# Keys of the cross attention by products with the weights stationary, and a second input scaled on GpSimd before its transposes

## The reference, cut to what matters

```python
h = rmsnorm(x, norm_xattn_g[i])
m = rmsnorm(mem.astype(dt), norm_mem_g[i])
q = (h @ xattn_wq[i].astype(dt)).reshape(bsz, seq, XATTN_HEADS, XATTN_HEAD_DIM)
k = (m @ xattn_wk[i].astype(dt)).reshape(bsz, -1, XATTN_HEADS, XATTN_HEAD_DIM)
v = (m @ xattn_wv[i].astype(dt)).reshape(bsz, -1, XATTN_HEADS, XATTN_HEAD_DIM)
s = jnp.einsum('bshd,bmhd->bhsm', q, k).astype(f32) * (XATTN_HEAD_DIM ** -0.5)
p = jax.nn.softmax(s, axis=-1).astype(dt)
o = jnp.einsum('bhsm,bmhd->bshd', p, v).reshape(bsz, seq, D_MODEL)
```

## Time and profile before

| what | value |
|---|---|
| median of the runs | 1251.29 us |
| profiled execution, its own time | 1251.01 us |
| span of the profiled execution | 1249.8 us |
| TensorE busy | 1240.9 us, 99% of the span |
| VectorE busy | 814.7 us |
| ScalarE busy | 691.5 us |
| GpSimd busy | 140.7 us |
| granted TensorE clock, mean | 0.999 of full speed |

### The profile page before, as it was taken

The page is one execution under the profiler, slowest core; times in us unless marked ns, Lnnn a source line. Parts: engine busy times, 40 slices in busy tenths (PEclk is TensorE's granted clock), DMA queues, the critical chain, the costliest instruction groups (busy, mean ns, idle before and its releaser), DMA issues.

```text
span 1249.8 us, 17456 instructions
## 1 busy us (share of the span) xinstructions
PE 1240.9 (99%) x7066; PEld 1032.7 (83%) x7066; DVE 814.7 (65%) x1114; ACT 691.5 (55%) x1046; POOL 140.7 (11%) x119
## 2 busy tenths in 40 slices
PE   9999999999999999999999999999999999999997
PEld 7888888888888888888888887888888888888886
DVE  5657755566788556655567878746875765755654
ACT  6665644443778645444447765556855364655543
POOL 1130000000231200000000332000320000211112
PEclk9999999999999999999999999999999999999999
DMA  8755466865454657655545534333456543565652
GB/s 299 230 155 185 149 222 202 267 187 163 151 164 160 215 156 250 195 178 180 177 153 186 184 120 150 122 104 101 136 197 240 170 151 126 168 218 174 205 171 85
DMA packets 127697, 220.18 MB, mean 176 GB/s; under 512 B 8336, under 2 KB 71184, under 8 KB 127616
## 3 DMA queue, kind: packets, MB, share of 16 engines
q1 hardware_dynamic: 123360, 205.95, 51.1%
q0 software_dynamic: 2672, 10.20, 2.4%
q10 hardware_dynamic: 1584, 2.92, 0.6%
HBM read 215.88 MB, written 3.15 MB: 175 GB/s over the span
## 4 chain that ended last, share of the span: by engine, by line
PE 96%; issue 1%; DMA 1%; ACT 1%; DVE 0%; POOL 0%; ACTq 0%; SPq 0%; POOLq 0%
PE ps L403 25%; PE ps L405 25%; PE ps L404 25%; PE ps L503 5%; PE ps L507 2%; PE ps L823 1%; PE ps L420 1%; PE ps L680 1%; PE ps L811 1%; PE ps L1076 1%; PE ps L1061 1%; PE ps L782 0%; DMA ar<-in_mem 0%; PE ps L610 0%; DMA raw<-in_w_gate_up 0%
## 5 line engine op out<-in xcount | busy, mean ns | idle before, releaser
L1618 DVE TENSOR_TENSOR spl<-raw,spl 128x1024 fp32r<-128x1024 f32 x387 | 476.7, 1256 | 100.4 <-ACT spl L1109 99.0
L1109 ACT CAST spl<-raw 128x1024 fp32r<-128x1024 f32 x387 | 400.1, 1050 | 177.4 <-PE ps L405 88.3
L403 PE MATMUL ps<-spl,xs 128*128 128x512 f32 x928 | 371.5, 400 | 0.0
L405 PE MATMUL ps<-spl,xs 128*128 128x512 f32 x928 | 362.4, 391 | 0.0
L404 PE MATMUL ps<-spl,xs 128*128 128x512 f32 x928 | 361.8, 390 | 0.0
L405 PEld LDWEIGHTS ps<-spl,xs 128*128 128x128 f32 x928 | 174.3, 188 | 37.1
L403 PEld LDWEIGHTS ps<-spl,xs 128*128 128x128 f32 x928 | 174.5, 188 | 35.6 <-issue 1.5
L404 PEld LDWEIGHTS ps<-spl,xs 128*128 128x128 f32 x928 | 174.7, 188 | 34.1 <-issue 0.5
L403 PE MATMUL ps<-spl,ys 128*128 128x512 f32 x496 | 198.5, 400 | 0.1
L405 PE MATMUL ps<-spl,ys 128*128 128x512 f32 x496 | 193.7, 391 | 0.0
L404 PE MATMUL ps<-spl,ys 128*128 128x512 f32 x496 | 193.4, 390 | 0.0
(11 more groups left out here) (329 smaller groups left out, 1152.2 us busy)
## 6 DMA issues: line engine op xcount, KB each, us to landing
raw<-in_w_in SPq DMA_DIRECT2D x112, 512.0 KB, 3.9
raw<-in_w_gate_up SPq DMA_DIRECT2D x176, 256.0 KB, 4.0
raw<-in_mlp_w SPq DMA_DIRECT2D x64, 512.0 KB, 4.4
raw<-in_w_down SPq DMA_DIRECT2D x44, 512.0 KB, 4.4
raw<-in_w_out SPq DMA_DIRECT2D x24, 512.0 KB, 4.2
raw<-in_xattn_wk SPq DMA_DIRECT2D x8, 512.0 KB, 3.9
raw<-in_xattn_wv SPq DMA_DIRECT2D x8, 512.0 KB, 4.4
raw<-in_w_branch_gdn SPq DMA_DIRECT2D x8, 512.0 KB, 3.3
```

The lines of the kernel that those rows point to most:

```text
L403: self.do.matmul(bank, xh, hi, start=start, stop=False)
L405: m = self.do.matmul(bank, xl, hi, start=False, stop=stop)
L1109: self.do.copy(self.k.spl[:, u % NH, 0, :], self.k.raw[:, u % NR, :]).then_inc(*self.up("hi", (u,)))
L1618: self.do.tensor_tensor(lo, self.k.raw[:, u % NR, :], hi.bitcast(F32), ALU.subtract).then_inc(*self.up("lo", (u,)))
```

## The change

Keys: `kept()` no longer makes the two key blocks with tokens on partitions. A new `keys(i)` makes each from four `cols_joined` units (of 512 x 256 instead of 256 x 512 weights), and after every second one `key_sums` copies one half of PSUM on ScalarE and adds the other on VectorE. So what is stored and loaded back already has features on partitions, `kept_turn` with its 16 transposes is gone, and the scores wait for the load. The stores of the two key blocks come one step later.

Second input: joined products have the rows of `mem2` on the free axis, where a factor for each row can't be applied while PSUM is emptied. So `mem2` itself is scaled: at step 2 ScalarE takes the squares, VectorE adds the epsilon and GpSimd takes the power and multiplies the 128 x 1024 tile, for each of the two row tiles. The transposes at steps 6 and 7 wait for that. The squares at step 8 are gone, and the values are copied instead of scaled when PSUM is emptied.

```diff
     def xa_scores(self, p, t):
-        self.wait_ge(*self.at("am", "xt", "k", p, 1))
+        self.wait_ge(*self.at(f"ld_kv{p}", 0))
...
     def keep(self, i):
-        self.wait_ge(*self.at("ev", f"x{i}", 1))
+        if i < 2:
+            self.wait_ge(*self.at("dm", f"xk{i}", 1, 1))
+        else:
+            self.wait_ge(*self.at("ev", f"x{i}", 1))
...
+    def mem2_scale(self, t):            # ScalarE
+        self.wait_ge(*self.at("ld_mem2", 0))
+        self.fresh("sqm")
+        if t:
+            self.wait_ge(*self.at("sq", "mem2", 0))
+        self.do.activation(self.s("sqm"), self.s(f"mem2{'ab'[t]}"), ACT.Square,
+                           accum_out=self.small(f"ss_mem2{t}", 1)).then_inc(*self.up("sq", ("mem2", t)))
+
+    def key_sums(self, i, p):           # ScalarE
+        for f in range(2):
+            self.wait_ge(*self.at("mm", f"xk{i}", p, f))
+            self.fresh(f"x{i}")
+            self.do.copy(self.s(f"x{i}")[:, (2 * p + f) * T:(2 * p + f + 1) * T],
+                         self.ps((f"xk{i}", p), f)[:, T:2 * T]).then_inc(*self.up("am", ("xkc", i, p, f)))
...
+    def mem2_scale(self, t):            # VectorE
+        self.factor("mem2", t)
+
+    def key_sums(self, i, p):           # VectorE
+        for f in range(2):
+            c = self.s(f"x{i}")[:, (2 * p + f) * T:(2 * p + f + 1) * T]
+            self.wait_ge(*self.at("am", "xkc", i, p, f))
+            self.do.tensor_tensor(c, self.ps((f"xk{i}", p), f)[:, 0:T], c, ALU.add).then_inc(*self.up("dm", (f"xk{i}", p, f)))
...
+    def mem2_scale(self, t):            # GpSimd
+        v = self.s(f"mem2{'ab'[t]}")
+        self.factor("mem2", t)
+        self.wait_ge(*self.at("rs", "mem2", t))
+        self.do.tensor_tensor(v, v, self.small(f"r_mem2{t}", 1).to_broadcast([P, D]), ALU.mult).then_inc(*self.up("pm", ("mem2", t)))
...
     def second():
+        E.take("sqm")
+        for t in range(2):
+            E.mem2_scale(t)
+        E.give("sqm", ("sq", "mem2", 1))
+        yield
         for p in range(4):
-            E.turn_in("mem2", lambda E, t, p: (E.s(f"mem2{'ab'[t]}"), ("ld_mem2", 0)), p)
+            E.turn_in("mem2", lambda E, t, p: (E.s(f"mem2{'ab'[t]}"), ("pm", "mem2", t)), p)
             if p % 2:
                 yield
         for t in range(2):
-            E.squares_in("mem2", lambda E, t, p: (E.s(f"mem2{'ab'[t]}"), ("ld_mem2", 0)), t, f"mem2{'ab'[t]}")
-            E.give(f"mem2{'ab'[t]}", ("sq", "mem2", t))
-        yield
+            E.give(f"mem2{'ab'[t]}", ("tp", "in", "mem2", 3))
+
+    def keys(i):
+        for p in range(2):
+            for k in range(2):
+                E.cols_joined((f"xk{i}", p), at_half(W["xattn_wk"], 512 * i + 256 * p), k, "ys", tiles("mem2"))
+                if k:
+                    if not p:
+                        E.take(f"x{i}")
+                    E.key_sums(i, p)
+                E.ahead()
+                if i and (p, k) == (0, 0):
+                    keep(0)
+                yield
...
-         (second(), (6, 7, 8)), (ma, (15, 16, 17, 19, 22, 22, 25, 27, 29)), (norm, (29, 30, 31, 32)),
+         (second(), (2, 6, 7)), (ma, (15, 16, 17, 19, 22, 22, 25, 27, 29)), (norm, (29, 30, 31, 32)),
...
-        for i, n in enumerate(("xk0", "xk1", "xv0", "xv1")):
+        for i, n in enumerate(("xkT0", "xkT1", "xv0", "xv1")):
...
-    def kept_turn():
-        E.take("xkT0", "xkT1")
-        for i in range(2):
-            E.xa_turn("k", i, f"xk{i}", (f"ld_kv{i}", 0))
-            E.give(f"xk{i}", ("mx", "xt", "k", i, 1))
-            yield
...
-    plan(opening(E, "m1", W["w_branch_gla"], "xs", turned("yb")), (kept_turn(), (3, 4)))
+    plan(opening(E, "m1", W["w_branch_gla"], "xs", turned("yb")))
```

More of the change, by code:

```diff
@@ L1166, in evac @@
             self.fresh(blk)
-            self.wait_ge(*self.at("rs", n, t))
-            self.do.mul(self.s2(blk)[:, t, :], self.ps(blk, t),
-                        self.small(f"r_{n}{t}", 1)).then_inc(*self.up("ev", (blk, t)))
+            if n == "mem2":
+                a = self.do.copy(self.s2(blk)[:, t, :], self.ps(blk, t))
+            else:
+                self.wait_ge(*self.at("rs", n, t))
+                a = self.do.mul(self.s2(blk)[:, t, :], self.ps(blk, t), self.small(f"r_{n}{t}", 1))
+            a.then_inc(*self.up("ev", (blk, t)))
+    def mem2_scale(self, t):
[11 more added lines that the diff above has]
+                         self.ps((f"xk{i}", p), f)[:, T:2 * T]).then_inc(*self.up("am", ("xkc", i, p, f)))
     def squares(self, tag, v, n, ready, name):
@@ L2352 @@
 ahead turn turn_in squares_in norm_prep norm_scale rows_half acc_done evac gated gate_evac relu squares sums power factors merge let_merged
-up_sum up_relu warm load_first first_half load_ident load_rows load_tables load_second load_con load_gain load_slot load_kept load_narrow load_gate half weights keep
+up_sum up_relu mem2_scale key_sums warm load_first first_half load_ident load_rows load_tables load_second load_con load_gain load_slot load_kept load_narrow load_gate half weights keep
 mem_keys mem_keys_turn ma_norm ma_turn ma_scores softmax ma_sums eight ma_eight ma_out out_norm
@@ L2973, in second, with keep @@
         for t in range(2):
-            E.squares_in("mem2", lambda E, t, p: (E.s(f"mem2{'ab'[t]}"), ("ld_mem2", 0)), t, f"mem2{'ab'[t]}")
-            E.give(f"mem2{'ab'[t]}", ("sq", "mem2", t))
-        yield
+            E.give(f"mem2{'ab'[t]}", ("tp", "in", "mem2", 3))
[11 more added lines that the diff above has]
+                yield
+    def keep(i):
+        E.keep(i)
+        E.give(f"x{i}", (f"ld_st{i}", 0))
     def kept():
-        for i in range(4):
-            w = W["xattn_wv" if i > 1 else "xattn_wk"]
-            for k, _ in enumerate(block(E, f"x{i}", w, 512 * (i % 2), "ys", "mem2")):
+        for i in range(2):
+            yield from keys(i)
+        for i in range(2, 4):
+            for k, _ in enumerate(block(E, f"x{i}", W["xattn_wv"], 512 * (i % 2), "ys", "mem2")):
                 if k == 3:
-                    E.keep(i)
-                    E.give(f"x{i}", (f"ld_st{i}", 0))
+                    keep(i)
+                elif i == 2 and not k:
+                    keep(1)
                 yield
```

## The result

The changed kernel takes 1257.1 us (median of 6 runs, 1255.89 to 1258.21) against 1251.49 us for the kernel before (6 runs, 1250.8 to 1252.2): the ratio is 1.0043, with an interval of 1.0032 to 1.0055. It is slower by 0.4%, 5.6 us, where the forecast had 3.7 us. The profiled execution took 1257.37 us, with a span of 1256.1 us against 1249.8.

What follows compares the result with a forecast made beforehand. The prediction took TensorE's stream, busy 1240.9 of 1249.8 us, as the bound. Its terms, -1.74 + 0.3 + 4.0 + 1.1 = +3.7 us, gave 1255.0 us; own range 1253.3 to 1257, 8 in 10 1249.8 to 1258.3.

Steps and rivals of the forecast that it cites:

- The stream of TensorE: TensorE's own work: 16 transposes removed, -1.74 us, and 8 joined key units, +0.3 us; net -1.4 us.
- The scaling ahead of the transposes: Scaling `mem2` at step 2 delays GpSimd's and VectorE's work, so TensorE stalls 4.0 us, bounds 1.7 and 6.8.
- The prediction's own sign: Test on the changed kernel: no TensorE wait for GpSimd at step 6 (2 to 3 us expected) means the forecast is wrong.
- The splits are made four steps ahead, so that by itself costs nothing: VectorE's split of step 3 runs 2.9 us later, no sooner than 334.4, at no cost by itself.
- What TensorE meets at steps 6, 7 and 10: TensorE waits 2.5 us at `mem2`'s transposes; its shift is 3.4 us after group 0 and 4.0 us after group 1.
- The key sums: ScalarE's copies and VectorE's adds at steps 20 to 26 delay head 5's combination: 1.1 us, bounds 0 to 2.1.
- the 0.7 us of lead that I allowed for: At the key sums, ScalarE and VectorE come out of the earlier stretch some 0.7 us less late than TensorE.
- The rest: Later key stores, copied values and one more slot at step 2 each cost nothing; if wrong, some tenths of a us.
- A: Rival: multiplies finish before step 6 ends, at 1.5 us or less each, so nothing waits: -1.4 us, 1249.9; chance 0.15.
- B: Rival: stalls after the scaling are short and key sums hidden: +0.3 up to +2.5 us, about 1252.6; chance 0.21.
- C: Rival: contention makes one GpSimd multiply take 5 us, group 0's scaling ends 2.3 us later: 1257.5 to 1259; chance 0.12.
- D: Rival: joined key products cost another 1 us or so, banks being held for copy and add: 1256; chance 0.04.

Runs made afterwards that it cites:

- e3: The changed kernel without GpSimd's two multiplies, `mem2` turned unscaled, squares and powers kept at step 2: 1254.42 us, 1.0023 of the kernel before.
- e10: The changed kernel with the scaling of `mem2` at step 5 and its transposes at steps 8 and 9: 1259.37 us, 1.0056 of the kernel before.
- e1: The changed kernel with the new keys alone, `mem2` not scaled ahead and the keys left unscaled: 1252.45 us, 1.0004 of the kernel before.
- e5: e4 with the two blocks of values made ahead of those of keys: 1251.19 us, 0.9993 of the kernel before.
- e6: e4 with head 5's transposes one step later, at step 26: 1250.92 us, 0.9992 of the kernel before.
- e7: The changed kernel unedited, run and profiled again: 1256.92 us, 1.004 of the kernel before.
- e4: The changed kernel with the whole scaling of `mem2` moved into the first feed-forward part: 1252.23 us, 1.0004 of the kernel before.
- e2: The kernel before with only the scaling of `mem2` at step 2 and plain copies from PSUM, old keys: 1255.85 us, 1.0032 of the kernel before.

## Why the prediction was right in its outcome, and which step failed

**The stream of TensorE.** Predicted -1.74 for the transposes and +0.3 for the joined units; the shift falls by 1.8 us where the transposes stood. Right.

**The scaling ahead of the transposes.** The size was nearly right (4.0 us predicted, 4.4 measured), but by luck, since none of the three waits that made up the 4.0 us came, and one other wait, of 3.0 us, and 1.4 us behind it came in their place. The prediction's own sign, "If TensorE shows no wait for GpSimd at step 6, the forecast is wrong at its root", is met. The step that failed is "The splits are made four steps ahead, so that by itself costs nothing". It is true of the split. But the split is one instruction of VectorE's queue, and behind it stood the memory keys' scaling, finished 1.1 us before TensorE needed it (333.42 and 334.54). TensorE can even start when the first half is done, 0.46 us after the scaling starts (337.17 and 337.63); before, that was at 333.13, so the lead was 1.4 us. I asked who reads the delayed instruction and not who reads what is queued behind it. The delay that I had worked out myself, 2.9 us to 334.4 (334.65 measured), less 1.4 us would have given 1.5 us at L575, which is what e3 shows. Two more terms stand on it, neither of them in the prediction: GpSimd's first multiply holds the split for another 1.3 us, and the clock behind the gap costs 1.4 us.

The hold could have been read from the kernel before. One of its splits lasted 2.34 us, behind the only fast multiply of the earlier trace rows, which had begun 0.6 us earlier; a slow one, of 2.79 us, had begun inside a split (80.16 to 81.35).

```profile
80.33 2.79 POOL L2252 TENSOR_TENSOR ar<-ar,sml 128x1024 f32<-128x1024 f32 x1 [15.14 <-DVE sml L1738]
84.47 1.90 POOL L2252 TENSOR_TENSOR ar<-ar,sml 128x1024 f32<-128x1024 f32 x1 [1.36 <-DVE sml L1738]
```
```profile
85.11 2.34 DVE L1618 TENSOR_TENSOR spl<-raw,spl 128x1024 fp32r<-128x1024 f32 x1 [0.72 <-ACT spl L1109]
```

**What TensorE meets at steps 6, 7 and 10.** Predicted: waits of 2.5, 0.9 and 0.6 us (340.4 less 337.73 is 2.7, not 2.5; the shift of 3.4 us behind the second doesn't use it). None came. The chain on GpSimd was as I had it: powers and multiplies done at 339.7 (340.4 said), group 0's factors at 343.6 (343.4 said), although its power took 3.81 us and not 2.89. I had taken 2.89 "since VectorE then stands waiting", but a split of VectorE's had begun 0.17 us before the power (339.61 and 339.78). VectorE's scaling of group 0 waited 2.80 us and not some 5, as its own queue was late as well. But TensorE came 4.5 us late to each of these places, for which the rest was then ready: the second multiply ended at 339.67, and TensorE came at 342.23; group 0 was ready at 344.8, and TensorE came at 345.86. At its old time of 337.73 it would have waited 1.9 us for the multiply (an estimate from these two times). Delays on one path hide those behind them, and do not add up. e10 shows such a wait where nothing goes before it; e3 shows 0.4 us of the one for group 1.

**The key sums.** Predicted 1.1 us, bounds 0 to 2.1; measured 1.7: 1.4 us at head 5's transposes and 0.3 at L503, both at the places named. e1, without any disturbance before, has the same, and e5 and e6 take it away by the order alone. The mechanism was right, and so were the 2.1 us by which VectorE falls behind (its split of step 22 is at 402.74 instead of 396.27, 6.5 us, where TensorE was 4.5 us late). The term that failed is the 0.7 us of lead that I allowed for: at head 3 both engines came 4.5 us late.

**The rest.** No wait is at the stores, the copies or the slot. Not foreseen: the late loads of the cross attention's output weights, 1.2 us in the first profile and none in e7, of which it stays open whether the change has a part in them, and the 0.4 us at L680.

**Rivals.** A (-1.4 us) wanted 1.5 us or less for a multiply; both took 1.9 us. No wait for them came all the same, but only because TensorE was late already, and the time went up by that. B is out: e1 has the size that it gave, but only with the scaling left out. C gave 1257.5 to 1259 by one multiply of 5 us. The time, 1257.1, is nearly its own and the mechanism isn't: both multiplies took 1.9 us. What was held up was VectorE's split, which "VectorE itself waits here for GpSimd and leaves it alone" had excluded; that sentence holds from 339.8 on and not at 334. D falls: three joined units between the transposes of heads 3 and 4 cost 0.2 us more than the old ones (0.12 said), and no wait is for a bank that the additions hold.

The time lies in the range of 8 in 10, and 0.1 us above the forecast's own range. The sum was short by 1.9 us by the median and 2.6 us by the profiles: 0.6 for the key sums, 0.4 for the scaling, 0.4 at L680 and 1.2 for the late loads.

## What to carry to other kernels

Before putting work into an early step because its input is there, list for each engine that it passes what is queued behind it and by how much TensorE comes after that, not only who waits for the work itself; here the same squares, powers and multiplies cost some 4.9 us at step 2 and 6.5 us at step 5 (ratios less e4's, 0.0039 and 0.0052) and next to nothing in the feed-forward part. When a stall is found, count the clock behind it as well, and count each later wait only by what exceeds the delay already taken. A removal of work is worth its time only if its replacement stands where the engines that do it have a lead: 1.74 us of transposes were paid back by copies and additions that stood between two heads, and kept, if they are kept at all, with the values first (0.9993, which its interval does not tell from no change).

## What the runs showed of the hardware that was not expected

**The clock.** After idle times of TensorE of 2.84 us (the changed kernel), 2.9 (e7), 2.76 (e2) and 3.15 (e10), the granted clock was at 1.2 GHz for about 3.4 us; after 1.50 us (e3) and 1.36 us (head 5 of the changed kernel) no row shows a fall. In the changed kernel the fall came 0.4 us before TensorE went on, in the three others about 1 us after it, and TensorE was busy all the rest of that time. From L575 to L442 the changed kernel lost 1.4 us, e2 and e7 1.8 us, each with the 0.2 us that e3 has at full clock. So the wait of 2.84 us was worth 4.25.

**VectorE and GpSimd.** A split (VectorE, 128x1024, two inputs in SBUF) took 2.59 us where GpSimd's multiply had begun 0.4 us before it, and 1.22 us with that multiply gone. In the other order it is GpSimd that is slow: its power of 128x1 lasted 1.53 to 1.61 us beside a split, and 0.56 by itself. So in these rows the one that came second was held. In the kernel before 19 splits last 1.6 us or more, and at the start of each a GpSimd operation was already running. The Trainium skill ("GPSIMD Engine Reference", section 1, Specifications) says that the two share interfaces to SBUF and that GpSimd contends with VectorE's instructions of two SBUF inputs. By that rule the trace agrees: VectorE's reduction at 337.84, with one input, took its usual 1.21 us beside the second multiply. The small instruction at 339.08 also has one input and yet lasted 0.62 us instead of 0.18, until that multiply ended; the runs don't say why.
